# A hybrid attention and mLSTM layer on one core: another order of the first tiles' work and of the requests at both seams

## The reference, cut to what matters

```python
h = rmsnorm(x, g_pre); p = h @ w_in + b_in        # q,k,v,z (attention), q,k,v,o,z,i,f (mLSTM), g_a, g_b
att = sliding_window_attention(rope(q_a), rope(k_a), v_a, sinks, 16 meta keys)    # 16 heads, 4 kv heads, window 128
hm  = mlstm(q_m, k_m, v_m, i_m, f_m)              # 4 heads of 256, chunks of 128, matrix state C
y_a = att * silu(z_a); y_m = sigmoid(o_m) * hm * silu(z_m)
merged = sigmoid(g_a) * (y_a @ w_pa) + sigmoid(g_b) * (y_m @ w_pb)
x = x + rmsnorm(merged @ w_out, g_post)
```

## Time and profile before

| | |
|---|---|
| three runs | 2989.53, 2997.15, 2996.54 us, median 2996.54 |
| profiled execution | 2989.75 us, span 2987.9 us |
| mean granted clock of TensorE | 0.993 of 2.4 GHz |
| TensorE busy | 2917.9 us, 98% |
| VectorE, GpSimd, ScalarE busy | 50%, 46%, 35% |
| transfers | 473.93 MB, mean 159 GB/s |

### The profile page before, as it was taken

One profiled execution on the slowest core, in us unless ns is written; L12 is line 12 of the kernel. 1 busy time (PEld: TensorE's weight loads), 2 busy tenths in 40 slices (PEclk: granted clock), 3 DMA queues, 4 the chain that ended last, 5 costly groups with the idle time before them and its releaser, 6 DMA issues. The chain is left out here.

```text
span 2987.9 us, 48460 instructions
## 1 busy us (share of the span) xinstructions
PE 2917.9 (98%) x16584; PEld 2527.2 (85%) x16584; DVE 1483.6 (50%) x3709; ACT 1052.6 (35%) x2435; POOL 1365.8 (46%) x1430
## 2 busy tenths in 40 slices
PE   6999999999999999999999999999899999999998
PEld 5998998998997888788878887888688887878887
DVE  5665555554553333533353335333455655566587
ACT  4774544544543121311231122211233333333443
POOL 2224422422423555455545555454344435456576
PEclk9999999999999999999999999999999999999999
DMA  6442122122223643365436433633546666396843
GB/s 233 138 136 86 61 62 80 61 65 80 89 63 124 232 165 138 124 218 178 131 122 236 159 136 132 243 132 123 192 159 242 247 223 246 119 337 220 317 169 127
DMA packets 206053, 473.93 MB, mean 159 GB/s; under 512 B 21090, under 2 KB 75383, under 8 KB 201956
## 3 DMA queue, kind: packets, MB, share of 16 engines
q1 hardware_dynamic: 186308, 409.11, 39.6%
q10 hardware_dynamic: 16800, 52.54, 4.7%
q0 software_dynamic: 2720, 9.32, 1.0%
HBM read 316.49 MB, written 156.38 MB: 158 GB/s over the span
## 5 line engine op out<-in xcount | busy, mean ns | idle before, releaser
L312 POOL TENSOR_TENSOR a_all<-h_raw,a_all 128x256 fp32r<-128x256 f32 x548 | 397.1, 756 | 690.3 <-issue 446.7
L322 PE MATMUL bank_first<-w_all,a_all 128*128 128x384 f32 (+1 forms) x1088 | 415.7, 382 | 2.2 <-POOL a_all L312 2.2
L324 PE MATMUL bank_first<-w_all,a_all 128*128 128x384 f32 (+1 forms) x1088 | 395.0, 363 | 0.0
L323 PE MATMUL bank_first<-w_all,a_all 128*128 128x384 f32 (+1 forms) x1088 | 394.7, 363 | 0.0
L575 ACT ACTIVATE ml_qkt<-ml_pt 128x512 f32<-128x512 f32 x68 | 40.7, 598 | 908.2 <-PE ml_pt L881 908.2
L2601 DVE TENSOR_TENSOR a_all<-sums,a_all 128x512 fp32r<-128x512 f32 x163 | 179.3, 1101 | 166.2 <-ACT a_all L2475 165.1
L322 PEld LDWEIGHTS bank_first<-w_all,a_all 128*128 128x128 f32 x1088 | 204.5, 188 | 52.0 <-issue 28.4
L700 DVE TENSOR_TENSOR ml_qk<-bank_first,bias_all 128x512 f32<-128x512 f32 x67 | 46.3, 692 | 379.8 <-ACT ml_kw L579 370.9
L324 PEld LDWEIGHTS bank_first<-w_all,a_all 128*128 128x128 f32 x1088 | 204.4, 188 | 22.0
L323 PEld LDWEIGHTS bank_first<-w_all,a_all 128*128 128x128 f32 x1088 | 204.8, 188 | 19.9
L322 PE MATMUL bank_second<-w_all,a_all 128*128 128x512 f32 x544 | 220.7, 406 | 0.8 <-issue 0.8
(11 more groups left out here) (515 smaller groups left out, 7922.7 us busy)
## 6 DMA issues: line engine op xcount, KB each, us to landing
w_split<-w_early SPq DMA_DIRECT2D x140, 512.0 KB, 3.1
h_raw<-h_t SPq DMA_DIRECT2D x121, 512.0 KB, 4.5
w_all<-w_split SPq DMA_DIRECT2D x34, 1024.0 KB, 14.6
stage<-l_chunks_in SPq DMA_DIRECT2D x46, 512.0 KB, 6.8
w_rest<-w_split SPq DMA_DIRECT2D x16, 1024.0 KB, 9.8
w_early<-w_split SPq DMA_DIRECT2D x14, 1024.0 KB, 7.6
w_plain<-l_x_t_in SPq DMA_DIRECT2D x17, 512.0 KB, 6.1
h_t<-h_raw SPq DMA_DIRECT2D x17, 512.0 KB, 6.6
```

The lines of the kernel that those rows point to most:

```text
L312: q = nc.gpsimd.tensor_tensor(k.h_lo[:, u, j:j + 2], k.h_raw[:, u, j:j + 2], k.h_hi[:, u, j:j + 2].bitcast(F32), ALU.subtract)
L322: nc.tensor.matmul(out, hi[:, j], k.w_hi[:, j, col:col + n], start=(j == 0), stop=False)
L323: nc.tensor.matmul(out, hi[:, j], k.w_lo[:, j, col:col + n], start=False, stop=False)
L324: last = nc.tensor.matmul(out, lo[:, j], k.w_hi[:, j, col:col + n], start=False, stop=(j == KT - 1))
```

## The change

The stage's fifth chunk gets a buffer of its own (a cut of the array that later holds the low parts of the weights; square and diagonal move aside in it), so five chunks are requested in a row ahead of x of tile 1. The rotary tables get their own semaphore, and several later requests are reordered. ScalarE squares tile 1 after four chunk splits instead of before the first; VectorE makes tile 1's diagonal after chunk 1's split and its h after all five. In pass 0, tile 0, `normed(3)` stands before the masks. In mLSTM the requests at the start are rows, lmask, states, seqcol, bias, where they were states, bias, lmask, seqcol, rows; tile 1 of the first head too uses `first_bias`; GpSimd's first `prepare` waits for both tiles that read it. T3, B22 and T4 are all requested at the head of the last mLSTM slot.

```diff
 def stage_slot(k, c):
+    if c == STG:
+        return 2 * STG
 def staged(k, c):
+    if s == 2 * STG:
+        return k.stage_first
...
# mLSTM, SP
-            load_states(0)
-            load_bias(sp, 0)
-            sp.dma_start(lmask[:, :, :], k.c_lmask).then_inc(const_in[0], 16)
-            sp.dma_start(seqcol[:, :, :], k.c_seqcol).then_inc(const_in[1], 16)
             for n in range(2):
                 sp.dma_start(rows[:, n], ...).then_inc(rows_in[n], 16)
+            sp.dma_start(lmask[:, :, :], k.c_lmask).then_inc(const_in[0], 16)
+            load_states(0)
+            sp.dma_start(seqcol[:, :, :], k.c_seqcol).then_inc(const_in[1], 16)
+            load_bias(sp, 0)
...
             def slot(h, t, n, u, half):
                 load_h(...)
+                if h == MH - 1 and t == NPT:
+                    sp.wait_ge(proj_a, MH * NT)
+                    sp.wait_ge(proj_b, MH * NT)
+                    sp.wait_ge(proj_c, MH * NT)
+                    for block in (T3, B22, T4):
+                        for part in range(2):
+                            load_block(sp, k, 0, block, part, k.late_in[block][part])
...
# tail_weights
-                if t == NPT:
...
-                    for part in range(2):
-                        load_block(sp, k, 0, T3, part, k.late_in[T3][part])
...
# GpSimd, prepare
-                    pool.wait_ge(z_ready, 1)
+                    pool.wait_ge(z_ready, 2)
# VectorE, bias_of and evict_a
-                return k.first_bias if is_first(n, 1) else bias[:, h % 2]
+                return k.first_bias if is_first(n, 2) else bias[:, h % 2]
-                if is_first(n, 1):
+                if is_first(n, 2):
                     dve.wait_ge(k.first_bias_in, 80)
...
# attention, buffers
-        sq = k.w_plain[:, 1, 0:2, half_row]
-        diag = k.w_plain[:, 1, 2, half_row][:, 0:P]
+        k.stage_first = k.w_plain[:, 1, :, half_row][:, :, 0:P]
+        sq = k.w_plain[:, 1, 0:4, half_row][:, :, 2 * P:4 * P].rearrange("p (a b) n -> p a b n", a=2)
+        diag = k.w_plain[:, 1, 4, half_row][:, 2 * P:3 * P]
# attention, SP (the whole list after)
+            load_x(0); load_xt(0); chunks 0 to 4; load_x(1); load_xt(1); load_bias(0)
+            rcos, rsin (rope_in); load_x(2); load_cache(0); sink, sink4, headrow, meta_rep, meta_own (c_in)
+            load_xt(2); store_h(0); smask; amask (c_in); perm; load_x(3); store_h(1); load_xt(3)
...
# ScalarE
             square(0)
-            square(1)
-            act_split_chunk(nc, k, 0)
             act.wait_ge(gate_in[0], 16)
             nc.scalar.activation(k.w_hi[:, :, gate_cols], S["wif"][:], ACT.Copy).then_inc(gate_hi, 1)
+            for c in range(2):
+                act_split_chunk(nc, k, c)
             split_made(0, None)
-            act_split_chunk(nc, k, 1)
             for c in range(2, 4):
                 act_split_chunk(nc, k, c)
+            square(1)
+            act_split_chunk(nc, k, 4)
             split_made(1, None)
-            act_split_chunk(nc, k, 4)
             square(2)
             square(3)
# VectorE
             dve_split_chunk(nc, k, 0)
-            diagonal(1)
             dve.wait_ge(gate_hi, 1)
...
             dve_split_chunk(nc, k, 1)
-            normed(1)
+            diagonal(1)
             for c in range(2, 5):
                 dve_split_chunk(nc, k, c)
+            normed(1)
             diagonal(2)
...
-            dve.wait_ge(c_in, 16 * 8)
+            dve.wait_ge(rope_in, 32)
...
+                    if a == 0:
+                        normed(t + 3)
                     mask = amask[:, 0, :]
...
-                if a == 0 and t + 3 < NT:
+                if a == 0 and 0 < t and t + 3 < NT:
                     normed(t + 3)
# TensorE
-            for r in range(2):
-                scale_row(r)
+            scale_row(0)
             block_b(0, 0, 0, True)
+            scale_row(1)
             block_a(0, 0, 0, True)
             scale_row(2)
-            pe.wait_ge(c_in, 16 * 8)
+            pe.wait_ge(c_in, 16 * 6)
# tail, SP
-            for slot in (B22, T4):
-                for part in range(2):
-                    load_block(sp, k, 0, slot, part, late_in[slot][part])
```

More of the change, by code:

```diff
@@ L543, in tail_weights @@
                         load_block(sp, k, 0, B21, part, early_in)
-                if t == NPT:
-                    sp.wait_ge(proj_a, MH * NT)
-                    sp.wait_ge(proj_b, MH * NT)
-                    sp.wait_ge(proj_c, MH * NT)
-                    for part in range(2):
-                        load_block(sp, k, 0, T3, part, k.late_in[T3][part])
             def y_dram(h, t):
@@ L1082, in attention @@
         META = 3 * P
-        c_in, cache_in, order_in = sem("c_in"), [sem("cache_in0"), sem("cache_in1")], sem("order_in")
+        c_in, rope_in, cache_in, order_in = sem("c_in"), sem("rope_in"), [sem("cache_in0"), sem("cache_in1")], sem("order_in")
         proj_a, proj_b = sem("proj_a"), sem("proj_b")
@@ L1179, in _ @@
             load_xt(0)
-            for c in range(2):
+            for c in range(STG + 1):
                 load_chunk(sp, k, c)
@@ L1183, in _ @@
             load_xt(1)
-            for c in range(2, STG):
-                load_chunk(sp, k, c)
             load_bias(0)
+            sp.dma_start(rcos[:, :, :], k.c_rcos).then_inc(rope_in, 16)
+            sp.dma_start(rsin[:, :, :], k.c_rsin).then_inc(rope_in, 16)
             load_x(2)
-            load_xt(2)
-            sp.dma_start(rcos[:, :, :], k.c_rcos).then_inc(c_in, 16)
-            sp.dma_start(rsin[:, :, :], k.c_rsin).then_inc(c_in, 16)
+            load_cache(0)
             sp.dma_start(sink[:, :], k.sinks.to_broadcast([P, HEADS])).then_inc(c_in, 16)
@@ L1193, in _ @@
                          allow_slow_non_contiguous=True).then_inc(c_in, 16)
-            load_chunk(sp, k, STG)
-            load_x(3)
-            load_cache(0)
-            sp.dma_start(smask[:, :, :], k.c_smask).then_inc(order_in, 16)
             sp.dma_start(headrow, k.c_headrow).then_inc(c_in, 16)
-            sp.dma_start(amask[:, :, :], k.c_amask).then_inc(c_in, 16)
             sp.dma_start(meta_rep[:, :], k.c_meta_rep).then_inc(c_in, 16)
             sp.dma_start(meta_own[:, :], k.c_meta_own).then_inc(c_in, 16)
+            load_xt(2)
             store_h(0)
+            sp.dma_start(smask[:, :, :], k.c_smask).then_inc(order_in, 16)
+            sp.dma_start(amask[:, :, :], k.c_amask).then_inc(c_in, 16)
+            sp.dma_start(perm[:, :, :, :], k.c_perm).then_inc(order_in, 16)
+            load_x(3)
             store_h(1)
@@ L1210, in y_dram @@
                 return k.y_t[bass.ds(t, 1), :, JD * a:JD * (a + 1), :].rearrange("o p j n -> (o p) j n")
-            sp.dma_start(perm[:, :, :, :], k.c_perm).then_inc(order_in, 16)
             load_x(4)
@@ L1332, in square @@
                     act.wait_ge(rs_done, r - 1)
-                nc.scalar.activation(sq, x[u], ACT.Square, accum_out=ss[:, u:u + 1]).then_inc(sq_done, 1)
+                nc.scalar.activation(sq, x[u].rearrange("p a (b n) -> p a b n", b=2), ACT.Square, accum_out=ss[:, u:u + 1]).then_inc(sq_done, 1)
                 act.wait_ge(sq_done, r + 1)
@@ L2792, in hybrid_layer @@
         k.chunks, k.ML, k.AT = all_chunks()
-        k.landed, slot_total = [], [0] * (2 * STG)
+        k.landed, slot_total = [], [0] * (2 * STG + 1)
         for c, (m, _, _) in enumerate(k.chunks):
@@ L2839, in hybrid_layer @@
         k.h_lo = k.a_all[:, 1].rearrange("p (u i) j n -> p u (i j) n", u=2)
-        k.stage_landed = [sem(f"stage_landed{i}") for i in range(2 * STG)]
+        k.stage_landed = [sem(f"stage_landed{i}") for i in range(2 * STG + 1)]
         k.w_hi_ready = sem("w_hi_ready")
```

## The result

The changed kernel took 2975.93 us in the median of four runs (2973.22 to 2979.18), the kernel before 2994.57 us in the median of four beside it (2989.53 to 2997.15). The ratio is 0.9946, with a 95% interval of 0.9934 to 0.9958: 16.2 us less by the ratio, and between 12.6 and 19.8 (the two medians differ by 18.6). The forecast was 2978 us, from a sum of 18.0 us. The profiled execution took 2976.07 us, its span is 2974.2 us, 13.7 us under the span before.

What follows compares the result with a forecast made beforehand. TensorE, busy 98% of the span, was taken as the bound, with gains only where it waits: opening 4.15, first seam 4.6, second seam 9.2, sum 18.0 us off 2996.54, giving 2978 us, range 2967 to 2989.

Steps and rivals of the forecast that it cites:

- First projection at 18.3: Opening: TensorE's first projection starts at 18.3 us, 2.8 earlier than 21.15, most of it not kept.
- the 4.4 reckoned for the rule at its worst: Opening: if VectorE and GpSimd exclude each other, GpSimd's split takes 4.4 us, not 3.77, and the opening gains 3.5.
- Transposes at 32.3: Opening: TensorE's transposes come at 32.3 us instead of 33.44, 1.1 us gained.
- normed(3), 2.05: Opening: normed(3) ahead of the masks fills VectorE's idle time; 2.05 us gained, 1.7 of TensorE's wait stay.
- Clock behind it, 1.0: Opening, after the shortened 1.7 us wait: work may stay at 2.4 GHz; 1.0 us gained, taken between 0 and 2.
- First seam, 4.6: Attention to mLSTM: wait of 2.75 plus 2.14 for the low clock, less 0.3 for thin margins; 4.6 us gained.
- rival (d): First seam: states replace the bias as the wait; 1.5 us late brings back wait and perhaps low clock; 2981, chance 0.06.
- Second seam, 9.2: mLSTM to tail: early weights leave no wait, three products take 8.2 us instead of 17.47; 9.2 us gained.
- (a): Second seam: six requests hold SP past 2128.7, delaying stores and barrier; at 3 or 4 us 2982, chance 0.07.
- (b): Second seam: SP's block lasts until 2147 or more, making the kernel slower, 2997 to 3006; chance 0.02.
- Rival (e): Second seam: VectorE behind GpSimd causes the wait before T4's product; earlier weights save only about 3, 2985; chance 0.05.
- Rival (c): Opening gives nothing: x of tile 1 or 3 comes later than reckoned, or the clock falls again; 2982, chance 0.10.

Runs made afterwards that it cites:

- t3_early_only: On the kernel before, only T3's two requests at the head of the last slot, B22 and T4 still behind the barrier; ratio 0.9992 (0.9984 to 1.0001).
- order_no_normed3: On the kernel before, the opening's edits without moving normed(3); ratio 0.9993 (0.9984 to 1.0002).
- opening_only: On the kernel before, all of the opening's edits and nothing else; ratio 0.9987 (0.9978 to 0.9996), 3.9 us less.
- bias_only: On the kernel before, only tile 1's bias from the first buffer, with GpSimd's wait for two z, SP's order as before; ratio 0.9995 (0.9987 to 1.0004).
- t4_late: On the changed kernel, T4's two requests put behind the barrier again, T3 and B22 early; ratio to the kernel before 0.9947 (0.9934 to 0.9961).
- sinks_first: On the changed kernel, VectorE's three sink operations ahead of normed(2); ratio to the kernel before 0.9944 (0.9930 to 0.9957), median 2974.77 us.
- sp_order_only: On the kernel before, only SP's new request order at the first seam, tile 1's bias from the second buffer; ratio 1.0011 (1.0001 to 1.0021), 3.3 us slower.
- after_again: The changed kernel run once more with no edit; ratio to the kernel before 0.9947 (0.9933 to 0.9960).

## Why the prediction was right, and where not

The time came out 2 us under the forecast and inside the range; three places gained, each mainly by the mechanism that was given. That it came so near is partly luck. The forecast rests on a sum of 18.0 us, and the places give 14.3: 4.1 for the opening (4.15 forecast), 2.15 for the first seam (4.6) and 8.1 for the second (9.2). The medians of the first test happen to differ by 18.6. Point by point:

- **First projection at 18.3:** 18.14 to 18.79 in six profiles. x of tile 1 was expected at 18.4 and square(1) started at 17.96, so the 1 us allowed for chunk 4's short rows was about twice what they took. GpSimd's split took 3.76 beside VectorE's splits, as forecast, and not the 4.4 reckoned for the rule at its worst. But that doesn't speak against the exclusion itself (the Trainium skill, SBUF — State Buffer, Who interferes with whom). The single instructions show it, VectorE's in the trace of before, then VectorE's and the first of GpSimd's four parts in the changed kernel (window 14 to 16.1 us):

```profile
17.86 0.77 DVE L1530 TENSOR_TENSOR w_all<-scan_wif,w_all 128x64 fp32r<-128x64 f32 x1
18.55 1.76 DVE L206 TENSOR_TENSOR w_all<-stage,w_all 128x1024 fp32r<-128x1024 f32 x1
...
14.41 1.22 DVE L210 TENSOR_TENSOR w_all<-stage,w_all 128x1024 fp32r<-128x1024 f32 x1
14.49 1.72 POOL L316 TENSOR_TENSOR a_all<-h_raw,a_all 128x256 fp32r<-128x256 f32 x1 [9.16 <-ACT a_all L1344]
```

  In the changed kernel GpSimd's first part is 1.72 us long and the other three 0.71, and it ends 0.58 after VectorE's split: it fits a wait for that whole instruction. The sum is under 4.4 only because the gate split was over before GpSimd began, so that one split stood in its way and not two. Before, VectorE waited as well: its gate split took 0.77 instead of 0.22, chunk 1's 1.76 instead of 1.22.
- **Transposes at 32.3:** 31.8 to 32.7, mean 32.3. The gain of 1.1 was reckoned from 33.44, one of the earlier of eight profiles (32.93 to 35.56, mean 34.2); in the mean it is 1.9. With all of the opening's edits the stretch from there to the first mask is longer, 15.6 to 16.2 instead of 15.07, by the clock: 16 to 23 of the 24 matmuls of block_b ran at the low level, against 10 to 15 in the other profiles with the old order (t3_early_only apart, with 23 of them and 16.3 us). So at the masks 1.3 us are left (49.40 to 48.08 in the mean).
- **normed(3), 2.05:** 7.44 us from mask to perm matmuls became 5.38 in all five profiles that have it. The wait of 1.7 is 1.72. This number was the safest, since both ends hang on the same engine's work.
- **Clock behind it, 1.0: mis-sized, and not by the mechanism that was given.** From the perm matmuls to tile 1's transposes it is 5.46 to 5.75 in five of the six (7.24 in the sixth, t3_early_only) and 5.14 to 5.43 in the four: 0.3 us. I had hoped that after a wait of only 1.7 the clock would stay up. It was low in all five profiles with that wait: the 128x128 matmuls behind the perm matmuls take 0.42 us each, as they do before. And order_no_normed3, with the wait of 3.78, has 5.32, so the 0.3 does not come from normed(3). In the opening's mean of 4.1 us this part is 0.6, and nearly half of that is the one long stretch of t3_early_only; so it is luck, too, that 4.1 meets the forecast's 4.15.
- **First seam, 4.6: mis-sized, but not against its own profile,** where 4.28 came. The 2.75 us of wait and the low clock were those of one execution, in which the bias came late. And the low clock costs 1.55 and not 2.14: I compared a first round of 4.03 with a second of 1.89, but a first round takes 2.48 at full clock (930.64 to 933.12 in opening_only). 2.75 and 1.55 make the 4.3 that came. Seven profiles have that wait at 1.22, 1.37, 1.65, 1.72, 1.76, 2.39 and 2.75 us; behind the first five the clock stays up, and only the last two pay 1.5 more. What I had as bounds, 2 to 4.9, holds for another reason than I gave. Also, I named only the bias. A wait of 0.35 us for the rows stood in the trace of before, behind the bias's 8.89; bias_only shows that it is a second lock on the same door:

```profile
935.77 0.42 DVE L735 TENSOR_TENSOR ml_qat<-ml_qkt,ml_rows 128x256 f32<-128x256 f32 x1 [0.35 <-DMA ml_rows<-rows_t]
```

  Since the change moves both, the sum didn't suffer.
- **States, rival (d):** the margin is thinner than the 0.7 us reckoned. In two of the five profiles with both edits, t4_late and sinks_first, TensorE waits for them, 0.31 and 0.28 us. The clock doesn't fall.
- **Second seam, 9.2:** 9.3 us from the earlier trace rows to the two executions with full clock at the barrier (39.69 to 30.4), 7.7 to the three with the low one. **The step that was missing is that barrier:** "1.85 us of idle time, then work" was taken at the clock that it had in the profile before. In half of the profiles of the unchanged seam it was low as well (38.79 to 39.26 in all), and there it cost nothing, since TensorE then only came later to B22 and T4, which were late anyway: T4's product starts 17.9 to 18.1 us behind the barrier with the low clock and 18.2 to 18.5 with the full one. With the weights early nothing covers it, and it costs 1.6.
- **SP, rivals (a) and (b):** six requests end at 2116.7, on before's clock 2124.7, against 2127 reckoned, and the y store at 2127.3, which I hadn't counted as more than an issue. The margin was 0.6 us in this profile, where 0.8 was reckoned, and up to 1.05 in the three others with six requests. The barrier stood still for 1.85 as before.
- **Rival (e), VectorE behind GpSimd:** out by t4_late. My argument, that the landing at 2151.8 fits, was right. But t3_early_only shows how little one profile can tell here: VectorE's instruction and T4 both depend on transfers that end together.
- **Rival (c), the opening gives nothing:** out, by 4.1 us.

What stays open: why the medians of the first test differ by 18.6 and the places by 14.3. The attention stage alone spreads over 5 us between profiles, and both numbers lie within the interval. Nor do I know what sinks_first is worth; it is the fastest kernel in its batch but one, t4_late at 2974.18, and neither is told from the changed kernel.

## What to carry to other kernels

A wait for a transfer that one profile shows is one draw: here the same wait was 1.2 us in one execution and 2.75 in another, and the longer one also cost the clock. Take the gain of removing it as a range down to half, and read the place in every profile of a kernel that shares it before believing a term. When a stall is taken away, look for the next input of the same instruction chain, with its own small wait behind the large one (the rows behind the bias), and for what the stall had covered (the low clock behind the barrier). Of a batch of early requests, keep early only those that are late otherwise: T3 and B22 did all of the work here, T4's request at the barrier cost nothing and freed SP for 5 us.

## What the runs showed of the hardware

- After an idle time of 1.84 to 1.93 us at the barrier TensorE's next two products took 5.5 us in six of fourteen profiles (before, bias_only, sp_order_only, opening_only, after_again, t4_late) and 7.1 in the other eight, with the same work ahead of it. At the first seam five waits of 1.22 to 1.76 us were all followed by the full clock, and four of 2.39 to 4.10 us all by the low one.
- SP's issue of six requests of 1 MB in a row took 7.1 to 7.5 us, of four 2.5 (t4_late) and of two 0.9, with little else under way. Four at the barrier, beside a tile load of 1 MB, took 5.4 us (t3_early_only), and 6.5 to 7.2 where T3's 2 MB were under way as well (eight profiles). An estimate from these: SP goes on until about 4 MB are under way, and is held from there.
- A store of 128 KB behind the six took 2.58 us to issue in all four profiles that have them, instead of 0.32.
- GpSimd's subtraction and VectorE's splits, both with two inputs from SBUF, take turns: a part of GpSimd's that takes 0.71 us alone took 1.72 beside VectorE's split of 1.22, and a split of 1.22 took 1.76 beside GpSimd's.
